# Hybrid decoder trunk on one core: squares added on GpSimd, constants converted there, lambdas summed by TensorE, and the sum of squares one weight unit later

## The chip, the core and the metric

One core of one Trainium2 chip. The core has five engines that run their own instruction streams and meet at semaphores: TensorE (PE in the profile, with its weight loads as PEld), VectorE (DVE), ScalarE (ACT), GpSimd (POOL) and SyncE (SP, here the issuer of all DMAs). The metric is the device time of one launch in microseconds, the median of several runs; lower is better.

## The reference, cut to what matters

```python
for l in range(2):
    h = h + 0.5 * swiglu(rmsnorm(h), w1[l], w3[l], w2[l])          # FFN 1: 1024 -> 2816 -> 1024
    u = rmsnorm(h)
    z = u @ w_in[l]                                                # q, k, v of three branches, forget, gates
    lam = exp(sum(lq1 * lk1)) - exp(sum(lq2 * lk2)) + lam_init     # one number per layer, for branch A
    m = sum_i sigmoid(gate_i) * (attention_i @ proj_i)             # differential, forgetting, stick-breaking
    h = h + m @ w_out[l]
    h = h + 0.5 * swiglu(rmsnorm(h), ...)                          # FFN 2
return rmsnorm(h)                                                  # x is (1, 512, 1024) float32
```

`rmsnorm` needs, for each token, the sum of the squares of its 1024 values, and gives `1/sqrt(mean + eps)`, which the kernel calls `rstd`. Everything is float32.

## The kernel before, in words

**Layout.** `h` holds the 512 tokens as columns and the 1024 features as 8 blocks of 128 partitions. A product in full precision is made of three rounded ones (`three`, L663): each operand is split into a high half (rounded, made by ACT: `split` at L1138, `u_part` at L1147) and a low half (the rest, made by DVE: `split` at L1784 through `lo` at L1782, `u_part` at L1791). Weights stream from memory in units of 512 KB (`w_raw`, four places), are split into `w_hi`/`w_lo` (three places) and used by PE.

**An FFN** starts with six plain units (three gate units and three up units, banks 0 to 5 of PSUM): PE multiplies 8 blocks of one unit in `u_unit` (L672), 24 products each. I number them 0 to 5. Units 0 to 2 are split ahead; units 3, 4 and 5 are split inside `ffn` on ACT and DVE, when the place in `w_hi` is free. After the six, pairs of units go through a scheme that saves products by sums of halves: it needs, for the two halves of the tokens, differences and sums of `u` (`scaled`, `across`, `second`, `turned_sum`, `all_sum`, split by `..._hi` on ACT and `sum_lo` on DVE).

**The norm's path.** `h` is multiplied unnormalized; `rstd` is applied to the product. The squares are summed over the 8 blocks in `acc`, and then over the partitions by one product with ones on PE (`sum_of_squares`, L683, recorded at L686), in the old kernel after unit 1. ACT makes `rstd` of it with Ln and Exp (`norm`, L1157: L1161 and L1164). Only then can DVE scale the first gate (`plain_gate`, L1823), ACT do its SiLU (`silu`, L1166), and DVE form the hidden tile (`plain_up`, L1828). Each engine does its part in the order written: on ACT (L1325) `norm`, the table for SiLU, one high half, `silu`, then the split of unit 4; on DVE (L2136) the first gate, one low half, the first hidden tile, then the split of unit 4.

**Tables.** ACT's functions come in table sets; `preload_act_table_set` loads the one with Ln and Exp, `preload_act_table` the one with SiLU. Where the state at a loop's start isn't known, a load is put in by the compiler.

**The prologue** (before the loop over the two layers). SP issues in this order: lambdas, parameters, the first quarter of x, weight unit 0, the rest of x with a block of constants between, units 1 and 2, and two more blocks of constants (L522 to L538). PE runs 18 idle products on zeros (L1076) until the first unit is there. DVE multiplies and sums the lambda vectors, ACT takes the exponentials, DVE finishes them (L2702 to L2720). Then ACT and DVE make `u`, split units 0 to 2, ACT squares the 8 blocks and DVE adds them up (L1755 to L1761, L2735 to L2739), and ACT converts four constant blocks into their types (L1762 to L1766), which lie in the tiles that the first gates will overwrite.

**The loop body** is FFN 1, mixer, FFN 2; ACT's `ffn` begins with four `scaled` halves for the tokens of that FFN. After the loop, `norm` once more, and DVE multiplies the 8 output tiles (L2747), each of which SP stores.

Of the kernel before, what the change touches and what calls it, by code (L numbers as in the profile page):

```python
# [75 lines left out]
P_END = P_WF + DEPTH * ND * N_FOX  # L76
# [44 lines left out]
IDLE_PRODUCTS = 18  # L121
# [57 lines left out]
def trunk(nc, x, stream, params, lambdas, const, const_r, const_b, out):  # L179
    ctx = ExitStack()  # L180
    with ctx:
# [232 lines left out]
        def plain_tile(f):  # L414
            return tile(f)
# [10 lines left out]

        prob = [scratch[:, 2 * SEQ:2 * SEQ + TRI], scratch[:, 2 * SEQ + TRI:2 * SEQ + 2 * TRI]]
# [18 lines left out]
        lam_landed = sem("lam_landed")  # L446
# [25 lines left out]
        lam_in = sem("lam_in")  # L472
        lam_out = sem("lam_out")
# [43 lines left out]
        def _(sp):  # L517
# [4 lines left out]
            sp.dma_start(scratch[:, 5 * SEQ:6 * SEQ], lambdas).then_inc(lam_landed, 16)  # L522
# [119 lines left out]
        @block.gpsimd  # L642
        def _(pool):
            pool.memset(area[:, 0:SEQ].bitcast(F32), 0.0).then_inc(warm_set, 1)
            for layer in range(DEPTH):

                pool.wait_ge(forget_mm, layer + 1)
                pool.memset(q_rest(2, 0)[half(1), :].bitcast(F32), 0.0).then_inc(pads_set, 1)
                pool.wait_ge(pads_set, 4 * layer + 1)
                pool.memset(q_rest(2, 1)[half(0), :].bitcast(F32), 0.0).then_inc(pads_set, 1)  # L650
                for n, part in enumerate((PT_HI, PT_LO)):
                    pool.wait_ge(pads_set, 4 * layer + 2 + n)
                    zeros = area[:, part + PT_OFF[-1] - P:part + PT_OFF[-1]]
                    pool.memset(zeros.bitcast(F32), 0.0).then_inc(pads_set, 1)
# [3 lines left out]
        def _(pe):  # L658
# [121 lines left out]
            def ffn(order):  # L780
# [295 lines left out]
            for _n in range(IDLE_PRODUCTS):  # L1076
# [53 lines left out]
        def _(act):  # L1130
# [26 lines left out]
            def norm():  # L1157

                act.preload_act_table_set(LN_EXP)
# [16 lines left out]
            def scaled(k, gain, tail=False):  # L1176

                act.activation(whole(SCALED, k, tail), h_half(k, 1), ACT.Copy, scale=times(gain)).then_inc(u_hi_set, 1)

# [145 lines left out]
            def ffn(gain):  # L1325
                own = gain - ND
                scaled(0, own)
                scaled(1, own + 1)
                scaled(2, own + 2)
                scaled(3, own + 3)  # L1330
# [410 lines left out]
            act.wait_ge(lam_in, 1)  # L1741
            act.activation(lam[:, 4:8], lam[:, 8:12], ACT.Exp).then_inc(lam_out, 1)
# [11 lines left out]
            split(1, after=0)  # L1754
            act.activation(acc, h[:, 0:SEQ], ACT.Square).then_inc(acc_set, 1)  # L1755
# [6 lines left out]
            act.wait_ge(small_landed, 16 * 2)  # L1762
            hi(cst_b[:], scratch[:, 0:IN_BF16 * P])
            hi(cst_r[:], scratch[:, IN_BF16 * P:ROUNDED * P])
            hi(base_l[:], scratch[:, 1024:1024 + SEQ])
            hi(base_r[:], scratch[:, 1024 + SEQ:1024 + 2 * SEQ]).then_inc(const_set, 1)  # L1766
            with c.turns(0, DEPTH) as layer:
                ffn(layer * (3 * ND) + (P_GAIN + ND))
                mixer(layer, layer * (3 * ND) + (P_GAIN + 2 * ND))
                ffn(layer * (3 * ND) + (P_GAIN + 3 * ND))  # L1770
# [4 lines left out]
        def _(dve):  # L1775
# [360 lines left out]
            def ffn(gain):  # L2136
# [565 lines left out]
            dve.wait_ge(lam_landed, 16)  # L2702

            n = DEPTH * 2
            pairs = tile(4)[:, 0:n * HEAD]
            dve.tensor_tensor(pairs, SQ[:, 0:n * HEAD], SQ[:, n * HEAD:2 * n * HEAD], ALU.mult).then_inc(vec_done, 1)
            dve.wait_ge(vec_done, c.next(vec_done))
            dve.reduce_sum(lam[:, 8:8 + n], pairs.rearrange("p (a b) -> p a b", b=HEAD), AX_X).then_inc(lam_in, 1)
            dve.wait_ge(lam_out, 1)
            dve.wait_ge(par_landed, 16)  # L2710
# [120 lines left out]
def small_params(a):  # L2831
    p = np.zeros((P, P_END), np.float32)
    gains = []
    for n in range(DEPTH):
# [4 lines left out]
        p[:, P_WF + n * ND * N_FOX:P_WF + (n + 1) * ND * N_FOX] = wf.reshape(P, -1)  # L2839
    gains.append(a["final_norm"])  # L2840
    p[:, P_GAIN:P_GAIN + GAINS * ND] = np.stack(gains).reshape(GAINS * ND, P).transpose(1, 0)
    return p


def lambda_rows(a):

    rows = [a[f"diff_l{x}{m}"][n] for x in "qk" for n in range(DEPTH) for m in (1, 2)]
    return np.tile(np.concatenate(rows)[None, :], (P, 1))
# [22 lines left out]
```

## Time and profile before

| | us |
|---|---|
| median of 3 runs (2505.53 to 2506.16) | 2505.57 |
| the profiled execution's own time | 2503.49 |
| its span in the profile | 2501.7 |

| engine | busy us | share of the span | instructions |
|---|---|---|---|
| TensorE, products | 2478.0 | 99% | 15824 |
| TensorE, weight loads | 2248.1 | 90% | 15824 |
| VectorE | 2133.8 | 85% | 3881 |
| ScalarE | 1526.9 | 61% | 3061 |
| GpSimd | 4.4 | 0% | 13 |

A row of the timeline has the start, the duration, the engine, the line of the code, what is written and read, how many instructions are merged in it, and, in brackets, how long the engine was idle before it and what ended that. Instructions of one engine overlap at their ends, so that the distance of two starts is often shorter than a duration.

### The profile page before, as it was taken

To read this page: it belongs to the slowest core of one execution; us is meant where nothing else is said; L and a number is where in the kernel's file an instruction comes from. 1 tells how busy PE (TensorE), PEld (TensorE's weight loads), DVE (VectorE), ACT (ScalarE), POOL (GpSimd) and SP (SyncE) were. 2 spreads that over 40 slices of the span, in tenths; PEclk is the share of its full clock that TensorE was granted. 3 is DMA by queue.
4 is the path that set the end of the run, shared out by engine and by line. 5 is a ranking of instruction groups with operands and counts; after the bars stand their busy time and mean duration, and the time that the engine had idled before them with its cause. 6 is when DMAs were issued, how large, how long until landed. Compare 5 with 4: busy or idle time off the path is not lost.

```text
span 2501.7 us, 50059 instructions
## 1 busy us (share of the span) xinstructions
PE 2478.0 (99%) x15824; PEld 2248.1 (90%) x15824; DVE 2133.8 (85%) x3881; ACT 1526.9 (61%) x3061; POOL 4.4 (0%) x13
## 2 busy tenths in 40 slices
PE   8999999999999999999999999999999999999998
PEld 7999888888889989998889998888888898899987
DVE  8999868888888779998789997788888986799986
ACT  7666447777764456664466654578777554566643
POOL 0000000000000000000000000000000000000000
PEclk9999999999999999999999999999999999999999
DMA  4322321211123222223322223221111322223332
GB/s 157 110 108 101 110 102 60 68 60 60 66 91 106 93 102 101 101 101 118 111 94 101 101 96 128 82 68 60 68 60 60 111 93 101 94 101 110 108 110 102
DMA packets 65272, 235.88 MB, mean 94 GB/s; under 512 B 7232, under 2 KB 7488, under 8 KB 65088
## 3 DMA queue, kind: packets, MB, share of 16 engines
q1 hardware_dynamic: 65088, 233.64, 26.7%
q8 instruction: 90, 1.47, 0.2%
q14 instruction: 94, 0.77, 0.1%
HBM read 231.51 MB, written 2.10 MB: 93 GB/s over the span
## 4 chain that ended last, share of the span: by engine, by line
PE 91%; DVE 5%; issue 2%; ACT 1%; DMA 1%; DVEq 0%; SPq 0%; ACTq 0%
PE ps L665 28%; PE ps L666 28%; PE ps L667 28%; PE ps L906 2%; PE ps L837 1%; DVE w_lo L1782 1%; PE ps L826 1%; PE ps L880 1%; PE ps L879 1%; PE ps L828 1%; DVE area L1782 1%; PE ps L893 0%; PE ps L843 0%; PE ps L895 0%; DMA h<-x 0%
## 5 line engine op out<-in xcount | busy, mean ns | idle before, releaser
L1136 ACT ACTIVATE w_hi<-w_raw 128x512 fp32r<-128x512 f32 (+1 forms) x876 | 627.9, 723 | 474.4 <-PE ps L667 216.0
L1782 DVE TENSOR_TENSOR w_lo<-w_raw,w_hi 128x512 fp32r<-128x512 f32 (+1 forms) x876 | 703.1, 809 | 111.8 <-ACT w_hi L1136 96.0
L665 PE MATMUL ps<-u_hi,w_hi 128*128 128x256 f32 (+1 forms) x2432 | 787.7, 324 | 5.9 <-DVE w_lo L1782 3.2
L667 PE MATMUL ps<-u_hi,w_lo 128*128 128x256 f32 (+1 forms) x2432 | 780.8, 321 | 0.0
L666 PE MATMUL ps<-u_lo,w_hi 128*128 128x256 f32 (+1 forms) x2432 | 780.5, 321 | 0.0
L666 PE MATMUL ps<-area,w_hi 128*128 128x256 f32 (+1 forms) x1764 | 580.8, 329 | 0.0
L665 PEld LDWEIGHTS ps<-u_hi,w_hi 128*128 128x128 f32 x2432 | 463.3, 190 | 41.8 <-DVE w_lo L1782 4.5
L667 PEld LDWEIGHTS ps<-u_hi,w_lo 128*128 128x128 f32 x2432 | 463.2, 190 | 34.8
L666 PEld LDWEIGHTS ps<-u_lo,w_hi 128*128 128x128 f32 x2432 | 463.4, 191 | 32.6 <-issue 1.4
L665 PE MATMUL ps<-area,w_hi 128*128 128x256 f32 (+1 forms) x1400 | 480.0, 343 | 0.4 <-DVE h L1804 0.4
L667 PE MATMUL ps<-area,w_lo 128*128 128x256 f32 (+1 forms) x1400 | 477.6, 341 | 0.0
L666 PEld LDWEIGHTS ps<-area,w_hi 128*128 128x128 f32 x1764 | 335.3, 190 | 30.0 <-issue 0.5
L665 PEld LDWEIGHTS ps<-area,w_hi 128*128 128x128 f32 x1400 | 265.4, 190 | 32.7 <-issue 1.7
L667 PEld LDWEIGHTS ps<-area,w_lo 128*128 128x128 f32 x1400 | 265.3, 190 | 30.0
L665 PE MATMUL ps<-v_area,w_hi 128*128 128x256 f32 x880 | 250.0, 284 | 1.1 <-ACT scratch_whole L1218 1.0
L667 PE MATMUL ps<-v_area,w_lo 128*128 128x256 f32 x880 | 249.0, 283 | 0.0
L1218 ACT ACTIVATE scratch_whole<-ps 128x256 f32<-128x256 f32 x376 | 141.7, 378 | 161.7 <-PE ps L667 160.1
L1136 ACT ACTIVATE area<-scratch_whole 64x512 fp32r<-64x512 f32 (+4 forms) x338 | 179.6, 569 | 36.3 <-DVE scratch_whole L2620 11.8
L1782 DVE TENSOR_TENSOR area<-scratch_whole,area 64x512 fp32r<-64x512 f32 (+4 forms) x248 | 138.8, 584 | 42.1 <-ACT area L1136 39.4
L665 PEld LDWEIGHTS ps<-v_area,w_hi 128*128 128x128 f32 x880 | 168.8, 192 | 3.0 <-DVE w_lo L1782 2.1
L667 PEld LDWEIGHTS ps<-v_area,w_lo 128*128 128x128 f32 x880 | 168.9, 192 | 0.0
L666 PE MATMUL ps<-v_area,w_hi 128*128 128x256 f32 x440 | 124.5, 283 | 0.0
(188 smaller groups left out, 2915.1 us busy)
## 6 DMA issues: line engine op xcount, KB each, us to landing
w_raw<-weights SPq DMA_DIRECT2D x435, 512.0 KB, 3.6
h<-x SPq DMA_DIRECT2D x4, 512.0 KB, 8.3
out<-scratch_whole SPq DMA_DIRECT2D x8, 256.0 KB, 2.5
scratch_whole<-const_b SPq DMA_DIRECT2D x1, 512.0 KB, 10.2
scratch_whole<-const_r SPq DMA_DIRECT2D x1, 320.0 KB, 8.9
scratch_whole<-lambdas SPq DMA_DIRECT2D x1, 256.0 KB, 2.5
cst<-const SPq DMA_DIRECT2D x1, 137.0 KB, 7.9
par<-params SPq DMA_DIRECT2D x1, 94.0 KB, 2.6
```

The source lines that it names most:

```text
L665: pe.matmul(dst, hi, x_hi, start=start, stop=False, **kw)
L666: pe.matmul(dst, hi, x_lo, start=False, stop=False, **kw)
L667: return pe.matmul(dst, lo, x_hi, start=False, stop=stop, **kw)
L826: pe.matmul(dst, q_twice(branch, hd)[:, m], k_both(branch, hd)[:, 0:n], start=False, stop=False, skip_group_check=True)
L828: pe.matmul(dst, q_rest(branch, hd)[:, m], k_bias(branch, hd)[:, 0:n], start=False, stop=True, skip_group_check=True).then_inc(score_set, 1)
L837: last = pe.transpose(ps[:, SB0 + j, (i - j) * P:(i - j + 1) * P], prob[buf][:, at:at + P], ident)
L879: pe.matmul(ps[:, OB, SEQ - n:SEQ], v, w_hi_j, start=j == 0, stop=False)
L880: last = pe.matmul(ps[:, OB, SEQ - n:SEQ], v, w_lo_j, start=False, stop=j == NQ - 1)
L906: last = pe.matmul(ps[:, SB0 + j, width - n:width], negtri_r if i == j else negones_r, part, start=False, stop=i == NQ - 1, skip_group_che ...
L1136: return act.activation(dst, src, ACT.Copy)
L1218: act.activation(to, half_bank((of or banks(s))[2 if n == 1 else 0]), ACT.Copy).then_inc(snap_set, 1)
L1782: return dve.tensor_tensor(dst, src, hi_part.bitcast(F32), ALU.subtract)
```

## The change

- The lambda vectors come as 8 columns of the parameter block; their own DMA and input are gone. DVE multiplies them, one product of PE with ones (made by GpSimd in `lam_ones`) sums over the partitions, placed after the fifth idle product, and ACT takes the exponentials from PSUM. There are 15 idle products instead of 18.
- The seven additions of squares in the prologue and the four conversions of constants move to GpSimd. DVE waits for the conversions before its first gate.
- PE's sum of squares stands after unit 2 instead of unit 1, in all four FFNs.
- The four `scaled` halves move from the head of FFN 1 to the place before it: into the prologue, ahead of the squares, and to the end of the loop body, where they also run after the last layer. The table set with Ln and Exp is loaded at the head of FFN 1, not in its `norm`.
- In every FFN the split of unit 4 stands ahead of the first SiLU on ACT and ahead of the first hidden tile on DVE.

```diff
-IDLE_PRODUCTS = 18
+IDLE_PRODUCTS = 15
+        lam_ones = area_whole[:, SEQ:SEQ + P]
 @block.sync
-            sp.dma_start(scratch[:, 5 * SEQ:6 * SEQ], lambdas).then_inc(lam_landed, 16)
             sp.dma_start(par[:], params).then_inc(par_landed, 16)
 @block.gpsimd
             pool.memset(area[:, 0:SEQ].bitcast(F32), 0.0).then_inc(warm_set, 1)
+            pool.memset(lam_ones, 1.0).then_inc(warm_set, 1)
+            for d in range(1, ND):
+                pool.wait_ge(sq_set, d)
+                pool.wait_ge(acc_set, d)
+                pool.tensor_tensor(acc, acc, first_square(d), ALU.add).then_inc(acc_set, 1)
+            pool.wait_ge(small_landed, 16 * 2)
+            pool.tensor_copy(cst_b[:], scratch[:, 0:IN_BF16 * P])
+            pool.tensor_copy(cst_r[:], scratch[:, IN_BF16 * P:ROUNDED * P])
+            pool.tensor_copy(base_l[:], scratch[:, 1024:1024 + SEQ])
+            pool.tensor_copy(base_r[:], scratch[:, 1024 + SEQ:1024 + 2 * SEQ]).then_inc(const_set, 1)
 @block.tensor
                 u_unit(1, 1).then_inc(unit_done, 1)
-                sum_of_squares()
                 for f in range(1, PLAIN):
                     u_unit(2 * f, 2 * f % SLOTS).then_inc(unit_done, 1)
+                    if f == 1:
+                        sum_of_squares()
                     u_unit(2 * f + 1, (2 * f + 1) % SLOTS).then_inc(unit_done, 1)
...
                 pe.matmul(ps[:, 7, :], area[:, 0:P], area[:, 0:SEQ], start=True, stop=True)
+                if n == 4:
+                    pe.wait_ge(warm_set, 2)
+                    pe.wait_ge(lam_in, 1)
+                    pe.matmul(ps[:, 6, 0:2 * DEPTH], lam_ones, lam[:, 8:8 + 2 * DEPTH], start=True, stop=True
+                              ).then_inc(lam_mm, 1)
 @block.scalar
-            def norm():
-                act.preload_act_table_set(LN_EXP)
+            def norm(table=True):
+                if table:
+                    act.preload_act_table_set(LN_EXP)
...
-            def ffn(gain):
-                own = gain - ND
-                scaled(0, own)
...
-                scaled(3, own + 3)
+            def ffn(gain, first):
+                if first:
+                    act.preload_act_table_set(LN_EXP)
+                else:
+                    scaled_four(gain - ND)
...
-                norm()
+                norm(table=not first)
                 act.preload_act_table(ACT.Silu)
                 all_sum_hi(0)
+                split(1, raw=0)
                 silu(plain_tile(0))
-                split(1, raw=0)
...
-            act.activation(lam[:, 4:8], lam[:, 8:12], ACT.Exp).then_inc(lam_out, 1)
+            act.wait_ge(lam_mm, 1)
+            act.activation(lam[:, 4:8], ps[:, 6, 0:2 * DEPTH], ACT.Exp).then_inc(lam_out, 1)
...
             split(1, after=0)
+            scaled_four(P_GAIN)
             act.activation(acc, h[:, 0:SEQ], ACT.Square).then_inc(acc_set, 1)
...
-            act.wait_ge(small_landed, 16 * 2)
-            hi(cst_b[:], scratch[:, 0:IN_BF16 * P])
-            hi(cst_r[:], scratch[:, IN_BF16 * P:ROUNDED * P])
-            hi(base_l[:], scratch[:, 1024:1024 + SEQ])
-            hi(base_r[:], scratch[:, 1024 + SEQ:1024 + 2 * SEQ]).then_inc(const_set, 1)
             with c.turns(0, DEPTH) as layer:
...
-                ffn(layer * (3 * ND) + (P_GAIN + 3 * ND))
+                ffn(layer * (3 * ND) + (P_GAIN + 3 * ND), False)
+                scaled_four(layer * (3 * ND) + (P_GAIN + 3 * ND))
             norm()
 @block.vector
+                dve.wait_ge(const_set, 1)
                 plain_gate(0)
                 sum_lo(token_sum(ALL, 0), LAST, 0)
+                split(1, raw=0)
                 plain_up(0)
-                split(1, raw=0)
...
             split(1)
-            dve.wait_ge(acc_set, c.next(acc_set))
-            for d in range(1, ND):
-                add_square(first_square(d))
-                if d == 4:
-                    split(2)
+            split(2)
```

## Rows read from the trace of the kernel before

**Rows 1.** The page's first part: busy us, share of the span, instructions of each engine.
```profile
PE 2478.0 (99%) x15824; PEld 2248.1 (90%) x15824; DVE 2133.8 (85%) x3881; ACT 1526.9 (61%) x3061; POOL 4.4 (0%) x13
```

**Rows 2.** PE's waits over the span: us in total, times, longest us.
```profile
PE ps L665 <- DVE w_lo L1782: 3.2, 3, 2.0
```

**Rows 3.** Timeline of PE, 0 to 60 us.
```profile
3.10 7.23 PE L1077 MATMUL ps<-area 128*128 128x512 f32 x18 [3.10 <-issue]
10.34 0.49 PE L665 MATMUL ps<-u_hi,w_hi 128*128 128x512 f32 x1
...
17.09 0.50 PE L665 MATMUL ps<-u_hi,w_hi 128*128 128x512 f32 x1 [0.36 <-DVE w_lo L1782]
...
23.19 1.13 PE L686 MATMUL ps<-scratch_whole,cst 128*128 128x512 f32 x2 [0.38 <-DVE scratch_whole L1800]
...
38.42 0.50 PE L665 MATMUL ps<-u_hi,w_hi 128*128 128x512 f32 x1 [2.00 <-DVE w_lo L1782]
```

**Rows 4.** Timeline of ACT, 0 to 60 us.
```profile
13.44 1.34 ACT L1149 ACTIVATE u_hi<-h,par 128x512 fp32r<-128x512 f32 x2 [0.32 <-DMA h<-x]
...
15.68 0.62 ACT L1755 ACTIVATE scratch_whole<-h 128x512 f32<-128x512 f32 x1
...
20.80 0.51 ACT L1136 ACTIVATE cst_b<-scratch_whole 128x384 bf16<-128x384 f32 x1
...
22.67 1.28 ACT L1178 ACT_TABLE_LOAD   x1
23.97 1.71 ACT L1178 ACTIVATE area_whole<-h,par 128x256 f32<-128x256 f32 x4
...
29.96 1.28 ACT L1159 ACT_TABLE_LOAD   x1
...
36.07 1.04 ACT L1136 ACTIVATE w_hi<-w_raw 128x1024 fp32r<-128x1024 f32 x1
```

**Rows 5.** Timeline of DVE, 0 to 60 us.
```profile
22.44 0.69 DVE L1800 TENSOR_TENSOR scratch_whole<-scratch_whole,rstd 128x512 f32<-128x512 f32 x1
24.65 1.67 DVE L1849 SCALAR_TENSOR_TENSOR area_whole<-h,par,area_whole 128x256 f32<-128x256 f32 x4 [1.52 <-ACT area_whole L1178]
...
34.80 0.69 DVE L1826 TENSOR_TENSOR scratch_whole<-ps,rstd 128x512 f32<-128x512 f32 x1
...
37.14 1.23 DVE L1782 TENSOR_TENSOR w_lo<-w_raw,w_hi 128x1024 fp32r<-128x1024 f32 x1 [0.26 <-ACT w_hi L1136]
```

**Rows 6.** Timeline of SP's queue, 0 to 60 us.
```profile
0.73 0.40 SPq L522 DMA_DIRECT2D scratch_whole<-lambdas  x1
1.19 0.42 SPq L523 DMA_DIRECT2D par<-params  x1
```

**Rows 7.** Stretches: length, busy us by engine (instructions), granted clock, DMA share, GB/s.
```profile
7.50:9.00 1.50, 1.50 (x5) 1.21 (x4) 0.47 (x1) 0.87 (x2) 0.00 (x0) 1.00 0.95 281
...
12.00:17.00 5.00, 4.53 (x19) 3.13 (x18) 4.75 (x8) 4.68 (x8) 0.00 (x0) 1.00 1.03 417
```

**Rows 8.** Timeline of PE, 3 to 6 us.
```profile
3.10 3.32 PE L1077 MATMUL ps<-area 128*128 128x512 f32 x7 [3.10 <-issue]
```

**Rows 9.** Timelines of PE, ACT and DVE at the start of FFN 2, layer 1.
```profile
918.65 1.02 PE L686 MATMUL ps<-scratch_whole,cst 128*128 128x512 f32 x2
...
919.71 0.69 ACT L1161 ACTIVATE rstd<-ps,cst 128x512 f32<-128x512 f32 x1 [0.73 <-PE ps L686]
...
922.38 0.42 ACT L1136 ACTIVATE area<-area_whole 128x256 fp32r<-128x256 f32 x1
...
924.88 1.23 DVE L1782 TENSOR_TENSOR w_lo<-w_raw,w_hi 128x1024 fp32r<-128x1024 f32 x1 [0.26 <-ACT w_hi L1136]
```

**Rows 10.** Timeline of POOL, 0 to 60 us.
```profile
0.74 0.53 POOL L644 MEMSET area<- 128x512 f32 x1 [0.29 <-POOLq L2865]
```

**Rows 11.** Timelines of ACT and DVE, 2485 us to the end.
```profile
2489.85 1.28 ACT L1159 ACT_TABLE_LOAD   x1
...
2493.12 5.38 DVE L2747 SCALAR_TENSOR_TENSOR scratch_whole<-h,par,rstd 128x512 f32<-128x512 f32 x8
```

More of the change, by code:

```diff
@@ L75 @@
 P_WF = P_FB + DEPTH
-P_END = P_WF + DEPTH * ND * N_FOX
+P_LAM = P_WF + DEPTH * ND * N_FOX
+P_END = P_LAM + 4 * DEPTH
 C_IDENT, C_ONES, C_SEL = 0, P, 2 * P
@@ L176, in turns, with trunk @@
         self.read()
-def trunk(nc, x, stream, params, lambdas, const, const_r, const_b, out):
+def trunk(nc, x, stream, params, const, const_r, const_b, out):
     ctx = ExitStack()
@@ L445, in trunk @@
         warm_set = sem("warm_set")
-        lam_landed = sem("lam_landed")
         par_landed = sem("par_landed")
@@ L472, in trunk @@
         lam_in = sem("lam_in")
+        lam_mm = sem("lam_mm")
         lam_out = sem("lam_out")
@@ L1075, in _ @@
             pe.wait_ge(warm_set, 1)
-            for _n in range(IDLE_PRODUCTS):
+            for n in range(IDLE_PRODUCTS):
                 pe.matmul(ps[:, 7, :], area[:, 0:P], area[:, 0:SEQ], start=True, stop=True)
+                if n == 4:
[3 more added lines that the diff above has]
+                              ).then_inc(lam_mm, 1)
             with c.turns(0, DEPTH) as _l:
@@ L1178, in scaled, with scaled_four @@
                 act.activation(whole(SCALED, k, tail), h_half(k, 1), ACT.Copy, scale=times(gain)).then_inc(u_hi_set, 1)
+            def scaled_four(own):
+                for k in range(4):
+                    scaled(k, own + k)
             def across_hi(k, tail=False):
@@ L1761, in _ @@
                     split(2, after=0)
-            act.wait_ge(small_landed, 16 * 2)
-            hi(cst_b[:], scratch[:, 0:IN_BF16 * P])
-            hi(cst_r[:], scratch[:, IN_BF16 * P:ROUNDED * P])
-            hi(base_l[:], scratch[:, 1024:1024 + SEQ])
-            hi(base_r[:], scratch[:, 1024 + SEQ:1024 + 2 * SEQ]).then_inc(const_set, 1)
             with c.turns(0, DEPTH) as layer:
-                ffn(layer * (3 * ND) + (P_GAIN + ND))
+                ffn(layer * (3 * ND) + (P_GAIN + ND), True)
                 mixer(layer, layer * (3 * ND) + (P_GAIN + 2 * ND))
-                ffn(layer * (3 * ND) + (P_GAIN + 3 * ND))
+                ffn(layer * (3 * ND) + (P_GAIN + 3 * ND), False)
+                scaled_four(layer * (3 * ND) + (P_GAIN + 3 * ND))
             norm()
@@ L2701, in _ @@
             c.skip(tail_read, 9)
[L2702 to L2708, printed above, removed]
+            dve.wait_ge(par_landed, 16)
+            n = 2 * DEPTH
+            dve.tensor_tensor(lam[:, 8:8 + n], par[:, P_LAM:P_LAM + n], par[:, P_LAM + n:P_LAM + 2 * n], ALU.mult
+                              ).then_inc(lam_in, 1)
             dve.wait_ge(lam_out, 1)
-            dve.wait_ge(par_landed, 16)
             for layer in range(DEPTH):
@@ L2734, in _ @@
             split(1)
-            dve.wait_ge(acc_set, c.next(acc_set))
-            for d in range(1, ND):
-                add_square(first_square(d))
-                if d == 4:
-                    split(2)
+            split(2)
+            c.skip(acc_set, ND)
+            c.skip(sq_set, ND - 1)
             with c.turns(0, DEPTH) as layer:
@@ L2839, in small_params @@
         p[:, P_WF + n * ND * N_FOX:P_WF + (n + 1) * ND * N_FOX] = wf.reshape(P, -1)
+    rows = [a[f"diff_l{x}{m}"][n] for x in "qk" for n in range(DEPTH) for m in (1, 2)]
+    p[:HEAD, P_LAM:P_END] = np.stack(rows, 1)
     gains.append(a["final_norm"])
@@ L2842, in small_params @@
     return p
-def lambda_rows(a):
-    rows = [a[f"diff_l{x}{m}"][n] for x in "qk" for n in range(DEPTH) for m in (1, 2)]
-    return np.tile(np.concatenate(rows)[None, :], (P, 1))
 def kernel(**inputs):
@@ L2860 @@
         "params": small_params(a),
-        "lambdas": lambda_rows(a),
         "const": c, "const_r": r, "const_b": b,
```

3 lines of the change are left out of this document (removed).

## The prediction, made before the changed kernel was run

> **What bounds the kernel now.** I read the page first: TensorE (PE) is busy 99% of the span, VectorE (DVE) 85%, ScalarE (ACT) 61%, GpSimd (POOL) 0% [rows 1]. So time can be won only where PE waits. The list of PE's waits is short; its largest wait after the start is on DVE at L1782, the low half of a weight split, with 2.0 us at once [rows 2]. In PE's timeline I looked for rows that carry an idle time. Nearly all of what the change can reach lies in the first 38.42 us: 18 idle products from 3.10 to 10.3, the first real product at 10.34, unit 1 at 17.09, the sum of squares at 23.19, and unit 4 at 38.42 behind the wait of 2.00 us [rows 3]. From there PE has no gap over 0.3 us for hundreds of microseconds. **The quantity to forecast is the start of unit 4 in the first FFN**, 38.42 us; each microsecond there is one in the end, unless it is given back at a later place that the change touches.
>
> Why 38.42? ACT's and DVE's timelines [rows 4, 5]. x lands whole at 13.44, ACT makes u, splits a weight unit, then squares until 20.8, converts constants until 22.67, loads a table, and only from 23.97 makes the scaled halves. DVE waits for these until 24.65, then works without a real gap until the first gate at 34.80 (10.15 us), whose SiLU must be over before ACT splits unit 4's weights (36.07) and DVE makes the low half (37.14 to 38.37). So the bound is ACT, then DVE, not PE.
>
> **The change, part by part.** Times are of the profiled execution (span 2501.7, own time 2503.49; the median of the runs is 2505.57, 2.08 more, and I carry that over).
>
> *Lambdas.* The DMA of 256 KB leaves the head of SP's queue: x and all weights behind it are issued 0.46 us earlier, the distance of its two first issues [rows 6]. In that stretch the DMA engines are 95% and more busy at 281 GB/s and above [rows 7], where 0.26 MB cost 0.26/0.3 = 0.87 us. The two overlap, so I take 0.7 us for the last piece of x (0.46 to 0.87). Behind it stand x, constants and weight units; all move forward. The new product needs params, which land about where lambdas did (3.3), a small multiply on DVE, and PE has 5 idle products before it (3.10 to 5.2 at 0.43 each: the first 7 products take 3.32 less the last one's overlap [rows 8]). PE therefore doesn't wait there. What queues behind the wait on PE is 10 idle products and the first unit. 5 x 0.43 + about 0.7 for the two passes of a four-column product (no row; a 128x512 sum of squares takes 0.87, so 0.1 to 0.9) + 10 x 0.43 ends at 10.1, where 18 products ended at 10.3. ACT's exp and DVE's six small steps then lie at 5.9 to 7.3, before x has landed: nothing.
>
> *ACT in the prologue.* x whole at 12.7; u and split 1 as before (2.24 us from landing to the first square) give 15.0. Four scaled halves now come first: 1.6 (four take 1.71 with the last one's tail [rows 4]) to 16.6. First five squares at 0.52: 19.2; split 2 to 20.25; three squares to 21.8. The four conversions, 20.80 to 22.65, are gone from ACT (1.85 us), and of two table loads of 1.28 (at 22.67 and 29.96) one stays. Table loaded at 23.1.
>
> *DVE in the prologue.* Its seven additions (0.73 each, 5.1 us) go to GpSimd. DVE waits for split 2's high half (20.3), makes the low half by 21.45, enters the loop (0.4, a guess; ACT's 0 to 0.3 of issue there bound it) and can start the differences at 21.9 instead of 24.65. Plus the same 10.15: first gate at 32.0. Then 0.6 for the gate, 0.35 for one low half, and 1.23 for the split of unit 4, which no longer stands behind the SiLU: **unit 4 at 34.3**.
>
> *PE.* Unit 1 at 17.09 - 0.7 = 16.4, unit 2 at 21.8 (a unit takes 5.45), its end 27.3. Sum of squares there (0.87), unit 3 to 33.6. ACT needs, from the start of the sum to the end of the high half of unit 4: Ln at +1.06, Exp, SiLU table to +3.7, one high half to +4.1, split to +5.15; DVE's low half to +6.42 [rows 9], so 33.7. Three chains end at 33.6, 33.7 and 34.3. The last one sets it: gain 38.4 - 34.3 = 4.1 us. It can't exceed 38.4 - 33.6 = 4.8.
>
> *GpSimd.* No row shows an addition or a copy on it. Its only full-width row is a memset, 0.53 us for 128x512 [rows 10]. From below an addition costs 0.53 (it writes as much); from above three times that, 1.6, if two inputs and the output are passed one after another. I take 1.1, the middle. The first pair of squares is ready at 17.7; 7 x 1.1 = 7.7 gives 25.4, against PE's need at 27.3: hidden, and the cover is worth 1.9 us. At 1.6 each it is 28.9, and PE waits 1.6. The four conversions at 0.5 to 1.1 (2 to 4.4) end at 27.4 to 33.3, and DVE's new wait before its first gate is at 32.0: hidden, except at the top of both ranges (1.3 late). Who waits behind that wait: the gate, all DVE splits, PE.
>
> The Trainium skill, GPSIMD Engine Reference (3.1 Elementwise), has an addition of 2048 fp32 columns at 4497 ns; an estimate from it is 1.2 us for 512, and the sum would come out the same.
>
> *Sum of squares one unit later, in all four FFNs.* In the other three, PE has no gap at unit 4 now. The new rstd chain is the +6.42 above; PE, with the sum one unit later, wants unit 4 at +0.87 + 5.45 = +6.32. The chain is late by 0.1, and a restart costs another 0.1: 0.2 each, **0.6 us lost** (0 to 1.2). Swapping split and SiLU is what makes it so short; without it 0.9 more would be added each time. Next is unit 5's split, at about +10.4 against PE's +11.8: covered by 1.4 us.
>
> *Scaled halves at the end of the loop body.* At the turn between the layers they overlap ACT's loop overhead; PE has 10 us of units in front there: nothing. After the last layer they are useless work on ACT ahead of the final norm: 1.6 us before the table load at 2489.85, so rstd ends at 2494.1 instead of 2492.5. DVE's output now starts at 2493.12 behind its own splits [rows 11]: **1.0 us lost** (0.9 to 1.1).
>
> **Sum:** -4.1 + 0.6 + 1.0 = -2.5. Span 2499.2, own time 2501.0, median 2505.57 - 2.5 = **2503.1 us**.
>
> **Rivals.** *DVE and GpSimd take turns at SBUF.* If a DVE instruction with two SBUF inputs can't run beside a GpSimd instruction, each of DVE's short ones (0.4 us) waits for a GpSimd one. Place: from DVE's split 2 (20.3) on, five additions and four conversions are left, 5 x 1.1 + 4 x 0.6 = 7.9 us of blocking; DVE's first gate goes to 39.9, unit 4 to 42.2: 3.8 later than before, with the other losses +5.4: 2511.0. It decides against the change from some 2.5 us of delay on. For it: DVE is on the setting chain exactly there. Against it: no row shows DVE slower beside GpSimd, but GpSimd does nothing beside DVE in this trace but memsets, so the trace is silent.
>
> The Trainium skill, SBUF — State Buffer (Who interferes with whom), says that such a DVE instruction and a GpSimd instruction that reads SBUF exclude each other, the second waiting whole. It is the rule that speaks most against this change; the trace cannot test it.
>
> *GpSimd is slow.* At 2 us an addition, acc is ready at 31.7, the sum starts 4.4 late, unit 4 at 38.1: gain gone, +1.3: 2506.9. For it: nothing bounds GpSimd's price from above but my factor three.
>
> *The gain is less than it says*: PE's first products run slow. If the pause for the new product keeps the products at 0.43 instead of 0.23 after 10 us (the granted clock reads 1.00 in both parts [rows 7], so only the durations tell them apart), each of the first costs 0.2; five or ten of them are mostly hidden by the wait for unit 1 (PE ends unit 0 at 15.7, the weights are there at 16.4). Cost up to 1.3: 2504.4.
>
> **Chances.** Forecast (chains as worked out, partial slowing of DVE included) 0.66; taking turns 0.18; slow GpSimd 0.11; slow first products 0.05. Of the forecast's own range, 2501.0 to 2505.0, the low end is the gain at its bound (-4.8, 0.2 more for the earliest landing of x, + 0.9: 2501.5) less half a microsecond for the spread of the runs (0.6), the high end 2 us of mutual hindrance. Up to the slow-GpSimd case and the milder half of the taking of turns the range is **2501.0 to 2509.0**. A measurement of this kernel tells about 0.2%, 5 us, from no change: faster by more needs over 5 us, more than the 4.8 of the place (0.03); slower by more is the harder half of the turns (0.11); within it 0.86.
>
> **What would show it.** Right: the profile after has x whole by 12.9, the first scaled half on ACT by 15.2, the difference on DVE by 22.3, GpSimd's last addition before 27, PE's unit 4 near 34.3, the first output step near 2494.1, and 0.2 us waits at the fourth unit of the other FFNs. Wrong: DVE's x4 groups longer than 1.67 us or with gaps while GpSimd is busy (turns); a PE wait before L686 at 27 (slow GpSimd); a DVE wait on GpSimd before the first gate (conversions); products of 0.43 pace beyond 10.3 (slow start).

## The result, and the profile after

The changed kernel takes 2509.35 us (median of 20 runs, 2506.71 to 2510.39) beside 2504.45 us for the kernel before (20 runs, 2501.16 to 2506.16): a ratio of 1.002, 95% interval [1.0014, 1.0026]. That is 4.9 us slower, where 2.5 us faster was forecast, and 0.35 us beyond the upper end of the range. The profiled execution took 2509.43 us, its span is 2507.5, 5.8 us longer than the span of before. One run of the kernel before, made beside later kernels, took 3144.88 us at a granted clock of 0.72 and is left out of every median below.

The page hardly shows it; compare it with [rows 1]: GpSimd works 17.0 us instead of 4.4, and TensorE's busy time *grew* by 3 us with one instruction fewer. Some products became longer; which ones is shown below.

```profile
PE 2481.0 (99%) x15823; PEld 2249.4 (90%) x15823; DVE 2132.6 (85%) x3873; ACT 1524.2 (61%) x3059; POOL 17.0 (1%) x25
```

The waits of TensorE (after; us in total, times, longest) point to two places. The largest wait for the low half of a weight was 2.0 us in [rows 2]; it is 4.2 us now. The second line is new: one wait of 2.2 us that the trace puts down to nothing, at the turn between the layers (from the end of the loop body for the first layer to its start for the second).

```profile
PE ps L679 <- DVE w_lo L1806: 4.4, 2, 4.2
PE ps L679 <- issue: 2.2, 1, 2.2
```

**The first place: GpSimd beside VectorE.** First GpSimd's timeline of the kernel after, then VectorE's, then TensorE's, all of the first 45 us.

```profile
16.46 1.29 POOL L653 TENSOR_TENSOR scratch_whole<-scratch_whole 128x512 f32<-128x512 f32 x1 [15.06 <-ACT scratch_whole L1786]
17.90 1.29 POOL L653 TENSOR_TENSOR scratch_whole<-scratch_whole,w_lo_whole 128x512 f32<-128x512 f32 x1
19.34 2.09 POOL L653 TENSOR_TENSOR scratch_whole<-scratch_whole,rstd 128x512 f32<-128x512 f32 x1
21.57 2.73 POOL L653 TENSOR_TENSOR scratch_whole<-scratch_whole 128x512 f32<-128x512 f32 x2
...
25.88 1.28 POOL L653 TENSOR_TENSOR scratch_whole<-scratch_whole,rstd 128x512 f32<-128x512 f32 x1
...
29.03 0.80 POOL L658 CAST base_r<-scratch_whole 128x512 f16<-128x512 f32 x1
```

```profile
20.20 5.82 DVE L1873 SCALAR_TENSOR_TENSOR area_whole<-h,par,area_whole 128x256 f32<-128x256 f32 x4
25.94 3.42 DVE L1879 SCALAR_TENSOR_TENSOR area_whole<-h,par,area_whole 128x256 f32<-128x256 f32 x4
29.28 2.01 DVE L1887 SCALAR_TENSOR_TENSOR area_whole<-h,par,area_whole 128x256 f32<-128x256 f32 x4
31.22 1.21 DVE L1806 TENSOR_TENSOR w_lo<-w_raw,w_hi 128x1024 fp32r<-128x1024 f32 x1
36.62 0.68 DVE L1850 TENSOR_TENSOR scratch_whole<-ps,rstd 128x512 f32<-128x512 f32 x1
```

```profile
27.20 1.12 PE L700 MATMUL ps<-scratch_whole,cst 128*128 128x512 f32 x2 [0.95 <-POOL scratch_whole L653]
32.48 0.80 PE L679 MATMUL ps<-u_hi,w_hi 128*128 128x512 f32 x1 [4.15 <-DVE w_lo L1806]
33.50 0.63 PE L681 MATMUL ps<-u_hi,w_lo 128*128 128x512 f32 x1
37.21 0.39 PE L681 MATMUL ps<-u_hi,w_lo 128*128 128x512 f32 x1
```

Read them against [rows 5]. The groups of four (x4) are differences and sums of halves; I call them all differences. They start at 20.20 instead of 24.65: the head start of 4.45 us is there, more than the 2.75 forecast. But the first four take 5.82 us where four took 1.67. From 20.20 to 31.22 the twelve differences last 11.0 us; at 1.6 from start to start, as in the kernel before, they are 4.8. Where GpSimd stops, at 29.8, VectorE is back at its own pace. GpSimd is held up too, though less: an addition lasts 1.29 us alone and 2.09 where it meets VectorE's low half of 18.93 to 20.27; behind that, its additions keep their 1.44 us from start to start (24.45 to 25.88), and VectorE gets one difference done in each. The head start is eaten, the weights of unit 3 are ready at 32.4, and TensorE waits 4.15 us before it.

**TensorE's clock.** Before [rows 3] TensorE waited too. What is new is what follows this wait: a product takes 0.63 us at 33.50 and 0.39 at 37.21. Stretches of the kernel after (length, TensorE's busy time and instructions, granted clock, DMA share, GB/s):

```profile
27.00:29.00 2.00, 1.12 (x2) 1.00 0.00 0
29.00:31.00 2.00, 0.00 (x0) 0.80 0.00 0
31.00:33.00 2.00, 0.52 (x1) 0.50 0.00 0
33.00:35.00 2.00, 2.00 (x6) 0.50 0.59 174
35.00:37.00 2.00, 2.00 (x6) 0.50 0.22 88
37.00:39.00 2.00, 2.00 (x10) 0.99 0.00 0
```

While the engine stood still, the granted clock fell from 1.00 to 0.50 (2.4 to 1.2 GHz), and it stayed there until 37, through 4.5 us of unit 3: some 2.2 us lost in that unit. Unit 4 starts at 40.18 instead of 38.42. VectorE had its low half ready at 38.8, so of these 2.2 us 1.4 are left at unit 4.

**The second place: the turn between the layers.** The same happens there, with a wait that the kernel before has too. First the kernel before, then after:

```profile
1252.56 0.49 PE L665 MATMUL ps<-u_hi,w_hi 128*128 128x512 f32 x1 [2.45 <-DVE u_lo L1794]
1250.00:1260.00 10.00, 7.55 (x34) 1.00 0.31 102
```

```profile
1254.67 0.49 PE L679 MATMUL ps<-u_hi,w_hi 128*128 128x512 f32 x1 [2.19 <-issue]
1255.77 0.63 PE L680 MATMUL ps<-u_lo,w_hi 128*128 128x512 f32 x1
1250.00:1260.00 10.00, 7.80 (x27) 0.83 0.35 122
```

A *shorter* wait, 2.19 us against 2.45, and yet the clock fell in this execution and not in that one: three units and a sum last 18.10 us, 1.63 more than in a kernel below whose clock stays at 1.00 there.

**The ledger** of the two profiled executions, at the same marks: unit 4 of the first FFN +1.76; the start of the second layer +2.11 (of it 0.25 at unit 4 of the first layer's FFN 2); after unit 4 of its first FFN +4.10 (1.63 of clock, 0.24 at unit 4); the last sum of squares +4.82; the first output step +5.83, of which 1.01 behind the last sum. 1.76 + 0.25 + 0.24 + 0.21 + 1.63 + 1.01 = 5.1 of 5.8. Of the other 0.7, 0.5 is a second step in the same three FFNs: some 20 us behind unit 4, at the first products that read `area` (952.44 in FFN 2 of the first layer), TensorE falls back by 0.16 to 0.18 us more.

### The profile page after: what moved, and what is told of

It reads as the page before. It is cut to its first block, busy times and chain, and to the rows that moved or that the text cites. A ratio compares the mean times of both kernels' runs of the same rounds, so it can differ in the third digit from the quotient of the medians.

```text
span 2507.5 us, 50060 instructions
## 1 busy us (share of the span) xinstructions
PE 2481.0 (99%) x15823; PEld 2249.4 (90%) x15823; DVE 2132.6 (85%) x3873; ACT 1524.2 (61%) x3059; POOL 17.0 (1%) x25
## 4 chain that ended last, share of the span: by engine, by line
PE 91%; DVE 5%; issue 2%; ACT 1%; DMA 1%; DVEq 0%; SPq 0%; ACTq 0%
PE ps L679 28%; PE ps L680 28%; PE ps L681 28%; PE ps L921 2%; DVE w_lo L1806 1%; PE ps L852 1%; PE ps L841 1%; PE ps L895 1%; PE ps L843 1%; PE ps L894 1%; DMA w_raw<-weights 1%; PE ps L908 0%; PE ps L858 0%; PE ps L910 0%; DVE area L1806 0%
## 5 line engine op out<-in xcount | busy, mean ns | idle before, releaser
L1806 DVE TENSOR_TENSOR area<-scratch_whole,area 64x512 fp32r<-64x512 f32 (+4 forms) x248 | 138.7, 583 | 42.2 <-ACT area L1157 39.4
```

Of the source, the lines that this page charges most:

```text
L1806: return dve.tensor_tensor(dst, src, hi_part.bitcast(F32), ALU.subtract)
```

## The experiments

**VectorE and GpSimd.** Two kernels undo one half each of what GpSimd was given, a third both. The first puts the additions back on VectorE:

```diff
-            for d in range(1, ND):                      # GpSimd
-                pool.wait_ge(sq_set, d)
-                pool.wait_ge(acc_set, d)
-                pool.tensor_tensor(acc, acc, first_square(d), ALU.add).then_inc(acc_set, 1)
...
+            dve.wait_ge(acc_set, c.next(acc_set))       # VectorE
+            for d in range(1, ND):
+                add_square(first_square(d))
+                if d == 4:
+                    split(2)
```

> The changed kernel with the seven additions of squares back on DVE, the four conversions still on GpSimd. Theory (DVE and GpSimd exclude each other while both read SBUF, and the long wait of PE that follows lets its clock fall): the four differences on DVE are back at 1.67 us (5.82 in the changed kernel), the conversions stretch some of DVE's additions instead, by at most 0.8 us each; unit 4 starts at 35.5 to 37 instead of 40.2, no PE wait over 2.5 us, granted clock 1.00 from 27 to 40; span 2502 to 2504 against 2507.5. Rival (the differences are slow for another reason, such as the halves' place in SBUF or the earlier DMAs): they still take 5 us and more, and unit 4 stays at 40 or later.

Measured: 2505.28 us (2503.42 to 2507.27, 10 runs) beside 2504.51, ratio 1.000 [0.9991, 1.001]. VectorE starts its differences later, at 23.98, and does four in 1.68 us:

```profile
23.98 1.68 DVE L1869 SCALAR_TENSOR_TENSOR area_whole<-h,par,area_whole 128x256 f32<-128x256 f32 x4 [0.59 <-DVE scratch_whole L1820]
36.35 0.50 PE L675 MATMUL ps<-u_hi,w_hi 128*128 128x512 f32 x1 [0.59 <-DVE w_lo L1802]
```

Unit 4 starts at 36.35, 3.8 us earlier than in the changed kernel. The engine that starts 3.8 us later ends earlier. GpSimd's conversions, now at 16.2 to 19.5, still lie beside VectorE's additions and stretch two of them (0.98 against 0.69 us). This execution also loses its clock at the turn, behind a wait of 2.48 us (0.83 in 1250 to 1260).

The second puts the four conversions back on ScalarE and leaves the additions:

```diff
-            pool.tensor_copy(cst_b[:], scratch[:, 0:IN_BF16 * P])          # GpSimd
...
-            pool.tensor_copy(base_r[:], scratch[:, 1024 + SEQ:1024 + 2 * SEQ]).then_inc(const_set, 1)
+            hi(cst_b[:], scratch[:, 0:IN_BF16 * P])                        # ScalarE
...
+            hi(base_r[:], scratch[:, 1024 + SEQ:1024 + 2 * SEQ]).then_inc(const_set, 1)
```

> The changed kernel with the four conversions back on ACT, the additions still on GpSimd. Theory: the first group of differences still takes 5 to 6 us, since the additions are what stands against it, the groups behind the last addition are at 1.67 us; unit 3 waits 3 to 4 us and the clock falls; span 2506 to 2508. Rival (the conversions are the costly part on GpSimd): differences at 1.67, unit 4 near 35, span 2502 to 2504.

Measured: 2508.47 us (2507.18 to 2509.86), ratio 1.0015 [1.0005, 1.0024]. The first four differences take 5.82 us as in the changed kernel, beside the additions; the next eight, which lay in part beside the conversions, take 2.69 and 1.66 instead of 3.42 and 2.01. The additions carry most of the harm, the conversions some 1 us of it.

The third does both edits:

> The changed kernel with both the additions (DVE) and the conversions (ACT) back, everything else of the change kept. Theory: no stretched instruction on DVE, differences start at 22.5 to 23.5, unit 4 at 35 to 36, clock 1.00 there; left are 0.24 us at unit 4 of each of three FFNs and 1.0 at the end, and up to 1.6 where the clock falls at the turn of the layers; span 2500 to 2502. Rival (the order of the sum and of the halves is what costs): unit 4 at 38 or later, span 2505 and more.

Measured: 2504.29 us (2503.01 to 2505.16), ratio 0.9998 [0.9989, 1.0008]. VectorE is undisturbed (four differences in 1.67 us from 23.03, 0.95 earlier than with the conversions on GpSimd, 0.3 of it an earlier head) and its split of unit 4 ends at 35.34. But an expectation was missed: the clock did not stay at 1.00 in the first FFN. Behind a wait of 1.84 us before unit 3 it fell (0.77 in 29 to 31, 0.50 in 31 to 33, 0.87 in 33 to 35), so that unit 4 came at about 36.1. No shorter wait here was followed by a fall.

*Is it exclusion of reads, or only GpSimd being busy?* In this kernel GpSimd fills 1280 columns with zeros in the place of each addition: about as long, but it reads nothing. It leaves the seven additions out, so it uses wrong sums.

```diff
-                pool.tensor_tensor(acc, acc, first_square(d), ALU.add).then_inc(acc_set, 1)
+                pool.memset(area_whole[:, 8 * SEQ:8 * SEQ + 1280], 0.0).then_inc(acc_set, 1)
```

> The changed kernel with each of GpSimd's seven additions replaced by a memset of 128x1280 elsewhere, about as long (1.3 us), with the same waits; the squares are not added up, so the norm of the first FFN is computed from the first block alone. Theory (only an instruction of GpSimd that reads SBUF stands against DVE): GpSimd is as busy as before, yet the differences on DVE take 1.67 to 2 us, and unit 4 starts at 34 to 36. Rival (any work of GpSimd hinders DVE, or it is not GpSimd): the first group still takes 5 us and more, unit 4 at 39 or later.

Measured: one run, 2502.52 us. Rows of GpSimd, VectorE and TensorE:

```profile
15.80 8.91 POOL L653 MEMSET area_whole<- 128x1280 f32 x7 [14.39 <-ACT scratch_whole L1786]
24.66 2.46 POOL L655 CAST cst_b<-scratch_whole 128x384 bf16<-128x384 f32 x1
```

```profile
19.43 1.67 DVE L1873 SCALAR_TENSOR_TENSOR area_whole<-h,par,area_whole 128x256 f32<-128x256 f32 x4
21.02 1.66 DVE L1879 SCALAR_TENSOR_TENSOR area_whole<-h,par,area_whole 128x256 f32<-128x256 f32 x4
...
25.33 1.41 DVE L1806 TENSOR_TENSOR v_area<-area_whole,v_area 128x256 fp32r<-128x256 f32 x4
26.67 2.75 DVE L1895 SCALAR_TENSOR_TENSOR area_whole<-h,par,area_whole 128x256 f32<-128x256 f32 x4
```

```profile
32.89 0.50 PE L679 MATMUL ps<-u_hi,w_hi 128*128 128x512 f32 x1 [0.42 <-DVE w_lo L1806]
```

Beside GpSimd's memsets VectorE runs at its own 1.67 us. From 24.66 on GpSimd reads, and the two meet again, but who is held up changes: up to 26.67 VectorE's low halves keep their pace (1.41 us for four) and the conversion, 0.70 us in the changed kernel, lasts 2.46; then four differences last 2.75 and the conversions keep their pace. What decides this stays open. So the two engines hinder each other where GpSimd reads SBUF, and not where it only writes. On VectorE's side every instruction that met a reading one here had two operands in SBUF; none with one was there to compare. The Trainium skill, SBUF — State Buffer (Who interferes with whom), states the rule for two SBUF inputs on VectorE against a GpSimd instruction that reads, and excepts one that only writes; the trace agrees, with 5.82 us beside reads and 1.67 beside memsets. It doesn't bear out that the two are apart for their whole length: in the changed kernel an addition and a difference together took 1.43 us from start to start (24.45 to 25.88), less than the 1.29 and 0.40 that they take alone.

Unit 4 comes at 32.89 here, earlier than the 34 to 36 expected and the 34.3 of the forecast. The head of this execution lies 0.64 us ahead of the changed kernel's (ScalarE splits unit 2 at 17.21 instead of 17.85), and the differences start at 19.43 instead of 21.9. From there to the first gate it takes 11.3 us: the 10.15 of the forecast, and 1.1 beside the conversions.

**TensorE's clock.** The next kernel gives TensorE 18 idle products in the wait before unit 3 of the first FFN of each layer:

```diff
                     if f == 1:
                         sum_of_squares()
+                        for _n in range(18 if order[0] == 0 else 0):
+                            pe.matmul(ps[:, 5, :], u_hi[:, 0:P], u_hi[:, 0:SEQ], start=True, stop=True)
```

> The changed kernel with 18 idle products (of u, into a bank that nobody reads) between the sum of squares and unit 3 in FFN 1 of each layer, where PE waits 4.2 us in the first layer. They fill that wait and change nothing else in the prologue. Theory (the wait lets PE's clock fall, and unit 3 runs at half speed up to 37): granted clock 1.00 from 27 to 40, unit 3 lasts 5.5 us, and unit 4 starts at 37.9 to 38.3 instead of 40.2, now set by DVE's split or by PE; in the second layer the products cost 18 x 0.23 = 4.1. Rival (the slow clock is due to something else, such as GpSimd's work): it falls as before, unit 4 at 40 or later.

Measured: one run, 2510.65 us; in the second layer, where nothing waits at that place, the idle products are a pure cost of about 4 us. In the first FFN the clock is 1.00 in all of 27 to 42, and

```profile
27.44 4.68 PE L806 MATMUL ps<-u_hi 128*128 128x512 f32 x18
...
38.50 0.50 PE L679 MATMUL ps<-u_hi,w_hi 128*128 128x512 f32 x1 [0.60 <-DVE w_lo L1808]
```

unit 4 starts at 38.50 instead of 40.18, waiting for VectorE again. The heads of these executions differ by themselves: ScalarE's split of unit 2 starts at 17.21 with memsets, 17.53 here and 17.85 in the changed kernel. Lined up at that mark, unit 4 comes at 33.53, 38.82 and 40.18. That splits the loss at unit 4: 5.3 us is the taking of turns with the additions, 1.4 us is the clock. (At its turn, behind a wait of 2.33 us, the clock did not fall.)

The same at the turn: the 8 idle products that stood behind the loop, ahead of the last sum, move to the end of the loop body and so also run between the layers.

```diff
                 ffn((2, 0, 1))
+                for _n in range(LAST_PRODUCTS):
+                    pe.matmul(ps[:, 0, :], area[:, 0:P], area[:, 0:SEQ], start=True, stop=True)
-            for _n in range(LAST_PRODUCTS):
-                pe.matmul(ps[:, 0, :], area[:, 0:P], area[:, 0:SEQ], start=True, stop=True)
             sum_of_squares()
```

> The changed kernel with the 8 idle products that stood after the loop moved to the end of the loop body, so that they also run at the turn between the layers, where PE waits 2.2 us and the granted clock then was 0.50 from 1255.8 to 1258.8. Theory (it is the wait that lets the clock fall there): clock 1.00 through the turn, the distance from the first to the second layer's unit 4 is 1.6 us shorter, span 2505.9 against 2507.5. Rival (the fall is not due to the wait): the clock falls as before, span as before.

Measured: 2507.42 us (2506.41 to 2507.96, 10 runs), 1.9 us below the changed kernel, ratio to before 1.001 [1.0001, 1.0019].

```profile
1252.69 1.98 PE L1104 MATMUL ps<-area 128*128 128x512 f32 x8
1254.91 0.49 PE L679 MATMUL ps<-u_hi,w_hi 128*128 128x512 f32 x1 [0.25 <-issue]
```

The idle products end before u is there, so they delay unit 0 by nothing, the clock stays at 1.00, and the sum of squares comes 16.47 us behind unit 0 instead of 18.10.

The same edit in the kernel *before*, whose runs spread from 2501 to 2506:

> The kernel before, with the 8 idle products of its end moved to the end of the loop body, so that they also run at the turn between the two layers, where TensorE waits 2.45 us. Theory: the clock falls behind that wait in some executions and not in others, which makes part of the spread of the kernel before (2501.2 to 2506.2); with the wait filled the clock stays at 1.00 at the turn, the upper part of the spread is gone, and the median is 1 to 2 us lower: 2502.5 to 2503.5, ratio 0.9992 to 0.9996. Rival: the spread comes from elsewhere; the median and the spread stay as they are (2504.5, over 4 us wide).

Measured: 2503.51 us (2501.50 to 2504.52, 10 runs) beside 2504.39 (2501.76 to 2506.34, 19 runs), ratio 0.9993 [0.9983, 1.0003]. The upper part of the spread is gone: 7 of the 19 runs of before are above 2505, none of these 10. The gain in the median, 0.9 us, can't be told from none. The profiled execution shows a second place where it happens or not. The kernel before waited 2.00 us at unit 4 of the first FFN and kept its clock [rows 3]; here, in the same code, it waited 1.97 and lost it:

```profile
37.88 0.50 PE L665 MATMUL ps<-u_hi,w_hi 128*128 128x512 f32 x1 [1.97 <-DVE w_lo L1782]
39.00:40.00 1.00, 1.00 (x5) 0.71 0.83 246
40.00:41.00 1.00, 1.00 (x3) 0.50 0.64 262
```

**The place of the sum of squares.** The changed kernel with the sum back behind unit 1, GpSimd's additions left as they are:

```diff
                 u_unit(1, 1).then_inc(unit_done, 1)
+                sum_of_squares()
...
-                    if f == 1:
-                        sum_of_squares()
```

> The kernel after, with the sum of squares back behind unit 1 in all four FFNs; GpSimd keeps its additions. My theory: the place of the sum is a trade. GpSimd's last addition ends at 27.2 as before, so TensorE stands still from the end of unit 1 (about 20.9) to 27.2, six microseconds instead of 1.0, and does units 2 and 3 behind it, partly at half speed; unit 4 starts at 41 to 42.5 instead of 40.2. In the three other FFNs the wait of 0.24 us before unit 4 is gone (0.7 less). Median 2509.5 to 2511.5. Rival: VectorE's and ScalarE's chain alone sets unit 4, so the place of the sum in the first FFN costs nothing; unit 4 at 40.2 or earlier, and 0.7 us are won: 2508.6.

Measured: 2508.12 us (2506.75 to 2508.97, 10 runs), ratio 1.0014 [1.0004, 1.0024]: my theory missed and the rival is nearer.

```profile
27.25 2.08 PE L700 MATMUL ps<-scratch_whole,cst 128*128 128x512 f32 x2 [6.30 <-POOL scratch_whole L653]
...
40.50 0.39 PE L679 MATMUL ps<-u_hi,w_hi 128*128 128x512 f32 x1
```

TensorE waits 6.30 us in one piece, and the clock falls, but most of the slow time lies in the wait itself (granted clock 0.64 in 23 to 24, 0.50 in 24 to 30, 0.95 in 30 to 31). Units 2 and 3 then run through without a gap, and unit 4 comes at 40.50, 0.3 later than in the changed kernel. In the three other FFNs both steps of the ledger are gone, at unit 4 and behind it: 0.38 us each, 1.1 in all. The turn, with a wait of 3.00 us, takes 0.8 of it back in this execution; the median is 1.2 below the changed kernel's, and the two intervals against before overlap. Setting the sum behind unit 2 bought 0.3 us at the head and cost 1.1 later.

**The lambda part alone**, in the kernel before: the parameters' columns, the product with ones, 15 idle products.

```diff
-            sp.dma_start(scratch[:, 5 * SEQ:6 * SEQ], lambdas).then_inc(lam_landed, 16)
...
+                if n == 4:
+                    pe.wait_ge(warm_set, 2)
+                    pe.wait_ge(lam_in, 1)
+                    pe.matmul(ps[:, 6, 0:2 * DEPTH], lam_ones, lam[:, 8:8 + 2 * DEPTH], start=True, stop=True
+                              ).then_inc(lam_mm, 1)
```

> The kernel before with the lambda part alone (columns of the parameters, product on PE, 15 idle products, no lambda DMA). Theory: the prologue moves forward as in the changed kernel, first unit at 8.7 (10.34 before), last piece of x 1.4 us earlier, and since DVE and ACT set unit 4 there, it starts at 36.6 to 37.2 instead of 38.4; span 2500 to 2500.5 against 2501.7. Rival (x's landing is hidden behind ACT's conversions or their DMAs): unit 4 stays near 38.4.

Measured: 2503.45 us (2501.93 to 2504.87, 10 runs) beside 2504.68 (27 runs), ratio 0.9995 [0.9986, 1.0005].

```profile
36.42 0.50 PE L668 MATMUL ps<-u_hi,w_hi 128*128 128x512 f32 x1 [2.00 <-DVE w_lo L1790]
```

Unit 4 starts 2.00 us earlier than in the profiled execution of before, 1.46 earlier than in the other one shown above (37.88, the same code up to there). ScalarE splits unit 1 at 12.72; the two executions of the old head have 14.72 and 14.17. This is the part of the change that works at its place: 1.5 to 2 us at the head. The medians differ by 1.2 us, and the interval doesn't tell that from none; this execution lost some 1.6 again at the turn, where the clock fell behind a wait of 2.18 us (0.83 in 1250 to 1260).

**What the experiments point to.** Lambda part, halves ahead of the squares and split ahead of the SiLU as in the change; additions on VectorE, conversions on ScalarE, sum behind unit 1 as before; the idle products at the turn; and the four scaled halves of the next FFN put where ScalarE is idle anyway, inside the last pair of FFN 2, instead of behind it:

```diff
@@ ScalarE, in down_hi, ahead of the last follow()
+                    if next_own is not None:
+                        scaled_four(next_own)
@@ ScalarE, end of the loop body
-                scaled_four(layer * (3 * ND) + (P_GAIN + 3 * ND))
@@ VectorE, down_vec
+                    if ends:
+                        dve.wait_ge(u_hi_set, c.peek(u_hi_set, 5))
```

> What the runs so far leave over: the lambda part, the halves ahead of the squares and the split of unit 4 ahead of the SiLU are kept; additions on DVE and conversions on ACT as in the kernel before; the sum of squares after unit 1 again; the halves for the next layer stand in ACT's idle 1.7 us before its last step of the last down pair instead of behind it; 8 idle products also at the turn of the layers. Theory: unit 4 of the first FFN at 35 to 36 (38.4 before), nothing lost at unit 4 of the other FFNs, the output steps start at the same distance from the last sum of squares as in the kernel before (3.1 us, 4.1 in the changed one), clock 1.00 at the turn; span 2498 to 2499.5, ratio 0.998 to 0.999 to the kernel before. Rival (gains in the prologue are lost to a fallen clock there): granted clock under 1.00 between 20 and 40, span 2500 and more.

Measured: 2500.41 us (2499.89 to 2501.16, 11 runs) beside 2504.68 (27 runs), ratio 0.9983 [0.9974, 0.9992].

```profile
35.89 0.50 PE L670 MATMUL ps<-u_hi,w_hi 128*128 128x512 f32 x1 [0.60 <-DVE w_lo L1801]
1249.96 0.49 PE L670 MATMUL ps<-u_hi,w_hi 128*128 128x512 f32 x1 [0.53 <-DVE u_lo L1813]
2487.22 1.13 PE L691 MATMUL ps<-scratch_whole,cst 128*128 128x512 f32 x2 [1.27 <-DVE scratch_whole L1819]
2490.43 5.38 DVE L2766 SCALAR_TENSOR_TENSOR scratch_whole<-h,par,rstd 128x512 f32<-128x512 f32 x8
```

It beats both kernels, by 4.3 and 8.9 us, and its eleven runs lie within 1.3 us. Its clock is 1.00 in 20 to 50 and in 1240 to 1270, and its output follows the last sum by 3.21 us, where the changed kernel needs 4.13. How the gain is shared among the parts was not measured one by one.

## Why the prediction was wrong, point by point

**The step that failed** is in *DVE in the prologue*: "plus the same 10.15". From the first difference to the first gate the changed kernel needs 16.4 us (20.20 to 36.62), because VectorE's differences and GpSimd's reading instructions held each other up; where GpSimd only writes in the place of its additions, it is 11.3 (19.43 to 30.70). The prediction had that case as a rival, with its place right (VectorE's differences beside five additions and four conversions) and its price nearly so: 7.9 us of blocking forecast, 11.0 - 4.8 = 6.2 measured, and 2511.0 against 2509.35. That the two totals lie so near is partly luck: the rival put unit 4 at 42.2 (40.18 measured) and had nothing for the clock. It gave it 0.18, with the reason that the trace was silent. That was the error of judgement. The silence of the trace speaks neither for nor against it, and the forecast's own sum put VectorE's longest row of two-operand instructions on top of GpSimd's reads. It also missed that the loss goes both ways: ScalarE's last square waits 1.52 us for a GpSimd addition, since the squares share places.

**The term that was missing** is TensorE's clock. A rival had a slow *start*; none had a fall behind a longer wait. It cost about 1.4 us before unit 4 and 1.6 at the turn, 3.0 of the 5.8 us between the two profiled executions. In the medians the turn counts for less, since the kernel before seems to pay there too in some executions: filling it brought 1.9 us in the changed kernel and 0.9, within its noise, in the one before. The time is 0.35 us beyond the range, so it would have stayed inside without this term.

**A wait that was overlooked.** The prediction calls 2.0 us TensorE's largest wait after the start. The kernel before waits 2.45 us at 1252.56, the turn. The prediction's "nothing" for that place held for the scaled halves (the turn itself came 0.25 us nearer), but it never asked what a wait of that length does to the clock.

**Terms that were sized wrongly.** A GpSimd addition: 1.1 us taken (0.53 to 1.6), 1.29 alone, 1.44 from start to start. The last of the seven ends at 27.2, so the cover of 1.9 us was gone and the sum waited 0.95. The lambda part: 0.7 us (0.46 to 0.87) taken, 1.5 to 2.0 measured at unit 4. Two executions of the old head differ by 0.5 by themselves, which the range of that term should have held; why x comes so much earlier than its 256 KB and one issue account for stays open. The bound "it can't exceed 4.8" rests on the same term and isn't one: with memsets the gain at unit 4 was 38.42 - 32.89 = 5.5, or 4.9 less the 0.64 of that execution's earlier head. The first difference was forecast at 21.9 and came at 20.20. The first real product was forecast at 10.1 (the terms given add up to 10.25) and came at 8.73: the ten idle products behind the new product took 2.87 us instead of 4.3.

The sum one unit later costs 0.25, 0.24 and 0.21 us at unit 4 of the other three FFNs, as forecast (0.2 each), but with the second step behind it 0.38 each: 1.1 instead of 0.6, inside the 0 to 1.2 that was given.

**Terms that held.** In FFN 2 of the first layer the chain from the sum to the end of the split takes 6.35 us (925.96 to 932.31), 6.42 as worked out from [rows 9], which shows the same place:

```profile
925.96 1.02 PE L700 MATMUL ps<-scratch_whole,cst 128*128 128x512 f32 x2
...
931.08 1.23 DVE L1806 TENSOR_TENSOR w_lo<-w_raw,w_hi 128x1024 fp32r<-128x1024 f32 x1 [0.53 <-ACT w_hi L1157]
```

The useless halves at the end cost 1.01 us (1.0), seen beside [rows 11] in the table load that now stands behind them:

```profile
2494.56 1.69 ACT L1200 ACTIVATE area_whole<-h,par 128x256 f32<-128x256 f32 x4
2496.27 1.28 ACT L1181 ACT_TABLE_LOAD   x1
...
2498.95 5.39 DVE L2767 SCALAR_TENSOR_TENSOR scratch_whole<-h,par,rstd 128x512 f32<-128x512 f32 x8 [0.92 <-ACT rstd L1186]
```

GpSimd's conversions took 2.7 us (2 to 4.4 taken) and were over at 29.8, before the first gate. And where GpSimd only writes in the place of the additions, VectorE's low half is the last thing unit 4 waits for (0.42 us), as the forecast had it.

## What to carry to other kernels

Before work moves to GpSimd, list what VectorE does in that same stretch: here its instructions with two operands in SBUF and GpSimd's reading ones held each other up, and when VectorE's stand on the path, the "free" engine is paid for by the busy one. Count a wait of TensorE not only by its length but by what the clock does behind it, and fill a wait of about two microseconds or more that can't be removed with idle products that end before its data come (the 4.2 and the 2.2 us filled here kept the clock at 1.00). Work that is only needed inside a loop belongs where the engine idles, not at the end of the body, where the last turn pays for it too.

## What the runs showed of the hardware

- *VectorE and GpSimd.* Four differences of 128x256 with two SBUF operands: 1.67 us alone and beside memsets, 5.82 beside GpSimd additions of 128x512, 2.75 beside its conversions. A conversion of 0.70 us lasted 2.46. The two overlap in part even so: an addition of GpSimd (1.29 us alone) and a difference of VectorE (0.40) took 1.43 us together.
- *TensorE's clock behind short waits.* The twelve traces hold 19 waits of 1.8 us and more behind which it can be read. It fell from 1.00 to 0.50 behind waits of 1.84, 1.97, 2.18, 2.19, 2.48, 2.52, 2.60 and 3.00 us and behind the four longer ones (3.06, 4.15, 4.16, 6.30), and not behind 1.89, 2.00 (twice), 2.01, 2.28, 2.33 and 2.45 us. So the length of a wait near 2 us does not decide it, and the same code fares differently from one execution to the next. In the eight short cases it fell between 0.5 us before and 1.5 us after the engine worked again, and the following products ran at half speed for some 3 us, which cost about 1.6 at the turn. What decides it is open; so is whether it makes all of the spread in the runs of the kernel before, of which filling the turn took the upper part.
